# Two transformer blocks on one core: weight splits moved ahead of the fill matmuls in the second block's mixers, two adds given to GpSimd, opening, norms and dense entry reordered

## What is computed

```python
h = h + 0.5 * rmsnorm(swiglu(rmsnorm(h, g1), w_gu, w_down), g2)
u = rmsnorm(h, mix_pre_g)
qa, ka, va, qb, kb, vb, qc, kc, vc, gl = split(u @ w_in)
oa = neighbourhood_attention(qa, ka, va)             # "na", 8 heads, bias table
ob = sliding_window_attention(rope(qb), rope(kb), vb) # "sw", 8 heads, sink
oc = differential_attention(rope(qc), rope(kc), vc)   # "diff", 4 heads, two maps each
merged = sum_n sigmoid(gl_n + b_gate_n) * (o_n @ w_branch_n)
h = h + rmsnorm(merged @ w_out, mix_post_g)
h = h + 0.5 * rmsnorm(swiglu(rmsnorm(h, g3), ...), g4)
```

## Time and profile before

| | us |
|---|---|
| median of 3 runs | 2783.58 (2783.43 to 2784.21) |
| profiled execution | 2782.96 |
| its span, first to last instruction | 2781.2 |
| PE busy in the span | 2564.1 |
| DVE, ACT, POOL busy | 1798.0, 1398.5, 193.8 |

### The profile page before, as it was taken

One profiled execution on the slowest core, in us unless ns is written; L12 is line 12 of the kernel. 1 busy time (PEld: TensorE's weight loads), 2 busy tenths in 40 slices (PEclk: granted clock), 3 DMA queues, 4 the chain that ended last, 5 costly groups with the idle time before them and its releaser, 6 DMA issues. The chain is left out here.

```text
span 2781.2 us, 32412 instructions
## 1 busy us (share of the span) xinstructions
PE 2564.1 (92%) x11950; PEld 2103.3 (76%) x11950; DVE 1798.0 (65%) x1716; ACT 1398.5 (50%) x1485; POOL 193.8 (7%) x270
## 2 busy tenths in 40 slices
PE   7899998699999999999799879889999998888998
PEld 5678776588888888888688767668878876766786
DVE  4564555588888988989654557765555455666553
ACT  3444444376767776777444435444444444443442
POOL 2100020000000000000230000010015000000100
PEclk9899998699999999999899989999999999999999
DMA  6355442289888988999575333345447533333551
GB/s 233 123 189 186 176 149 92 107 344 361 347 351 339 366 349 345 360 355 354 195 236 197 111 133 129 115 167 212 181 166 241 199 129 137 122 122 142 205 188 61
DMA packets 88119, 592.12 MB, mean 213 GB/s; under 512 B 11288, under 2 KB 11472, under 8 KB 20304
## 3 DMA queue, kind: packets, MB, share of 16 engines
q1 hardware_dynamic: 77456, 558.99, 53.0%
q0 software_dynamic: 10560, 31.74, 4.1%
HBM read 585.36 MB, written 5.32 MB: 212 GB/s over the span
## 5 line engine op out<-in xcount | busy, mean ns | idle before, releaser
L566 PE MATMUL pp<-hi_a,uT_hi 128*128 128x512 f32 x2224 | 901.3, 405 | 48.0 <-DVE uT_lo L1733 22.1
L568 PE MATMUL pp<-hi_a,uT_lo 128*128 128x512 f32 x2224 | 877.4, 395 | 0.0
L567 PE MATMUL pp<-lo_a,uT_hi 128*128 128x512 f32 x2224 | 877.3, 394 | 0.0
L1814 DVE TENSOR_TENSOR lo_a<-raw_a,hi_a 128x2048 fp32r<-128x2048 f32 x282 | 652.9, 2316 | 126.5 <-ACT hi_a L1297 126.5
L1297 ACT ACTIVATE hi_a<-raw_a 128x2048 fp32r<-128x2048 f32 x282 | 537.8, 1908 | 6.4 <-DMA raw_a<-in_moe_gu 5.9
L566 PEld LDWEIGHTS pp<-hi_a,uT_hi 128*128 128x128 f32 x2224 | 427.2, 192 | 138.0 <-issue 27.8
L568 PEld LDWEIGHTS pp<-hi_a,uT_lo 128*128 128x128 f32 x2224 | 426.0, 192 | 92.3
L567 PEld LDWEIGHTS pp<-lo_a,uT_hi 128*128 128x128 f32 x2224 | 428.0, 192 | 82.4
L567 PE MATMUL acc<-lo_b,hT_hi 128*128 128x512 f32 x792 | 311.9, 394 | 0.0
L1847 DVE TENSOR_TENSOR lo_b<-raw_b,hi_b 128x2048 fp32r<-128x2048 f32 x116 | 265.9, 2292 | 46.4 <-ACT hi_b L1315 45.3
L566 PE MATMUL acc<-hi_b,hT_hi 128*128 128x512 f32 x576 | 227.8, 395 | 10.8 <-DVE lo_b L1847 10.8
(11 more groups left out here) (251 smaller groups left out, 2806.7 us busy)
## 6 DMA issues: line engine op xcount, KB each, us to landing
raw_a<-in_moe_gu SPq DMA_DIRECT2D x176, 1024.0 KB, 6.3
raw_b<-in_moe_wd SPq DMA_DIRECT2D x88, 1024.0 KB, 8.4
raw_a<-in_ffn_w_gu SPq DMA_DIRECT2D x88, 1024.0 KB, 6.7
raw_a<-in_w_in SPq DMA_DIRECT2D x72, 1024.0 KB, 6.8
raw_b<-in_ffn_w_down SPq DMA_DIRECT2D x44, 1024.0 KB, 4.9
raw_a<-in_ffn_gu SPq DMA_DIRECT2D x22, 1024.0 KB, 5.9
raw_a<-in_w_out SPq DMA_DIRECT2D x16, 1024.0 KB, 5.9
raw_a<-in_w_branch SPq DMA_DIRECT2D x12, 1024.0 KB, 5.9
```

The lines of the kernel that those rows point to most:

```text
L566: nc.tensor.matmul(out_ap, l_hi, r_hi, start=start, stop=False, skip_group_check=True)
L567: nc.tensor.matmul(out_ap, l_hi, r_lo, start=False, stop=False, skip_group_check=True)
L568: return nc.tensor.matmul(out_ap, l_lo, r_hi, start=False, stop=stop, skip_group_check=True)
L1814: ins = nc.vector.tensor_tensor(lo_a[:, slot, cs], raw_a[:, slot, cs], hi_a[:, slot, cs].bitcast(F32), ALU.subtract)
```

## The change

1. **Tables.** `va` comes before `qk1` in `MIX`, `UNITS` is dealt out anew, and the splits move to other items and stand ahead of the item's units (the number in `SPLIT` says how many units stay ahead of them). The rotations of `kb`, `qb`, `qc`, `kc` come one item earlier and stand ahead of the item's units on DVE.

```diff
-MIX = (("in", "qk0", 512, 0), ("in", "qk1", 512, 512), ("in", "va", 512, 1024), ("in", "kb", 256, 1536),
+MIX = (("in", "qk0", 512, 0), ("in", "va", 512, 1024), ("in", "qk1", 512, 512), ("in", "kb", 256, 1536),
-UNITS = {"na": (1, 1, 1, ((3, 2), (2, 0), (2, 0), (2, 0), (2, 0), (2, 0), (2, 0), (2, 0))),
-         "sw": (1, 1, 1, ((1, 1),) * 8), "diff": (1, 1, 2, ((2, 1), (2, 2), (2, 1), (2, 1)))}
-SPLIT = {"na": (0, 1, 2, 4, 6), "sw": (0, 1, 3, 5, 7), "diff": (0, 1, 2, 3)}
-ROTATE = {"na": {5: "kb", 6: "qb"}, "sw": {2: "qc", 4: "kc"}, "diff": {}}
+UNITS = {"na": (1, 1, 1, ((2, 1), (2, 0), (2, 1), (2, 0), (2, 1), (2, 0), (2, 0), (2, 0))),
+         "sw": (1, 1, 2, ((0, 1),) + ((1, 1),) * 7), "diff": (1, 1, 2, ((2, 1), (2, 2), (2, 1), (2, 0)))}
+SPLIT = {"na": {1: 0, 2: 0, 4: 0, 6: 0, 7: 0}, "sw": {0: 0, 2: 0, 4: 0, 6: 0, 7: 1},
+         "diff": {0: 0, 1: 0, 2: 2, 3: 1}}
+ROTATE = {"na": {4: "kb", 5: "qb"}, "sw": {1: "qc", 3: "kc"}, "diff": {}}
```

In ACT's `mix` (DVE's `item` is changed alike):

```diff
-                        units(UNITS[kind][3][it][part])
+                        todo = UNITS[kind][3][it][part]
                         if part == 0 and it in SPLIT[kind]:
+                            units(SPLIT[kind][it])
+                            todo -= SPLIT[kind][it]
                             split()
+                        units(todo)
```

```diff
                     if kind == "diff":
-                        ins = nc.vector.tensor_scalar(s_o_, s_in, SCALE, None, ALU.mult)
+                        nc.vector.tensor_reduce(negmax[:, M % 4, :], s_in, AX_X, ALU.max, negate=True).then_inc(s_nm, 1)
+                        signal(s_sc)
+                        return
...
+                    src = acc[:, M % 2, tt * S:(tt + 1) * S] if kind == "diff" else sc[:, M % 2, tt, :]
```

```diff
                             if which:
                                 dve.wait_ge(s_fev, n["fev"])
-                                link(nc.vector.tensor_tensor(merged[:, tt, cs], merged[:, tt, cs], t[:, tt, cs], ALU.add))
+                                signal(s_part)
...
+                    g.wait_ge(s_part, n["added"])
+                    nc.gpsimd.tensor_tensor(merged[:, tt, cs], merged[:, tt, cs], t[:, tt, cs], ALU.add) \
+                      .then_inc(s_added, 1)
```

```diff
+                dve.wait_ge(s_ss, n["ss"])
+                link(nc.vector.tensor_tensor(merged[:, tt, :].rearrange("p (h c) -> p h c", h=2),
+                                             acc[:, 2 * tt:2 * tt + 2, :],
+                                             vec[:, slot, :].rearrange("p (h c) -> p h c", h=2), ALU.mult))
...
+                link(nc.vector.scalar_tensor_tensor(out=x[:, tt, :], in0=merged[:, tt, :], scalar=rstd[:, tt:tt + 1],
+                                                    in1=x[:, tt, :], op0=ALU.mult, op1=ALU.add))
```

```diff
+                        if opening and tt == 1:
+                            turn(Chunk(c.half, c.rest - 1))
...
-                    turn(Chunk(0, 0))
+                    if experts > 1:
+                        turn(Chunk(0, 0))
```

More of the change, by code:

```diff
@@ L530, in _ @@
             for i in range(N_LAYERS):
-                for j in range(2 if i else 0, D_IN // 512):
+                for j in range(2 if i else 1, D_IN // 512):
                     weight(wide(a["w_in"][i], 512 * j))
@@ L686, in gate_up @@
                     pe.wait_ge(s_alo, c.at(a0 + 1))
+                    opening = experts == 1 and isinstance(j, int) and j == 1
                     if c.rest == 0:
@@ L825, in qk @@
                     M = m0 + m
-                    if M >= 2:
+                    if kind == "diff" and m >= 2:
+                        pe.wait_ge(s_exp, n["exp"] + m - 1)
+                    elif M >= 2:
                         pe.wait_ge(s_sc, M - 1)
@@ L1396, in sb_sigmoids, with attend @@
                 nc.scalar.activation(z, z, ACT.Sigmoid).then_inc(s_keep, 1)
-            def attend(kind, between, behind, item):
+            def attend(kind, between, behind, item, turned=None):
                 maps = MAPS[kind]
@@ L1445, in attend @@
                 n["item"] += items
+                if kind == "diff":
+                    n["comb"] += items
             def mixer(l):
@@ L1978, in across, with attend @@
                 lo_tile(1, True)
-            def attend(kind, dst, ahead, item, done=None):
+            def attend(kind, dst, ahead, item, done=None, opening=None, early=None):
                 maps = MAPS[kind]
@@ L2089, in attend @@
                             scores(per * (it + 1) + m)
+                    if early and it < TT:
+                        early(it)
+                    if it + 1 < items:
                         if kind == "diff":
@@ L2314, in turn, with mix @@
                     rotate(projected(which)[1], 2 if which == "kb" else 8, which == "qb")
-                def mix(kind, dst, first=None, beside=None, done=None):
+                def mix(kind, dst, first=None, turned=None, done=None):
                     def ahead():
@@ L2335, in item @@
                                 signal(s_rope)
+                        units(todo)
                     n["g"] += 4
                     units(UNITS[kind][0])
-                    attend(kind, dst, ahead, item, done)
+                    attend(kind, dst, ahead, item, done, lambda: units(UNITS[kind][1]), turned)
                 def lambdas():
+                    link(nc.vector.tensor_scalar(pre_q, pre_rstd, SCALE, None, ALU.mult))
                     dve.wait_ge(s_lam, 80 * (l + 1))
@@ L2387, in mixer @@
                 link(nc.vector.tensor_scalar(nlam, nlam, -lam_init, None, ALU.add))
-                mix("diff", mixb[:, :, 1280:1792], beside=diff_beside, done=head_squares)
-                units(1)
+                mix("diff", mixb[:, :, 1280:1792], turned=lo_turned, done=head_squares)
+                wait_rstd()
+                gains["heads"] = gain()
+                for tt in range(TT):
+                    for h in range(3):
+                        head_norm(tt, h)
                 wait_rstd()
@@ L2393, in mixer @@
                     signal(s_rows)
-                for tt in range(TT):
-                    lo_turned(tt)
+                lo_half(1)
+                units(2)
+                lo_turned(0)
                 units(1)
                 signal(s_vecused)
+                lo_turned(1)
                 units(1)
```

198 lines of the change are left out of this document (113 added, 85 removed).

## The result

| | before | after |
|---|---|---|
| median us | 2783.51 (4 runs, 2781.55 to 2784.21) | 2697.42 (4 runs, see below) |
| profiled execution us, span | 2782.96, 2781.2 | 2695.91, 2693.9 |
| ratio after to before | | 0.969, interval 0.9671 to 0.9709 |

One of the four executions after was disturbed and took 14324.09 us: it counts in the median alone, while the ratio is that of the other three (2695.74 to 2698.93, the middle one 2695.91).

A forecast was written before the change was run, and what follows sets the result against it. PE was taken to bound the kernel, leaving its idle 217 us and low clock to win. Mixers 38, opening 5.1, norms 5.2 and dense entry 4.4 sum to 52.7, giving 2730.9 us, range 2712 to 2758.

The forecast's parts named there:

- The mixers: Second block's two mixers: of 54 us to win in each, 35.2 stay, so two give 38 us.
- the opening: Program start: PE starts its first weights 8.9 us earlier, of which 5.1 us are kept.
- norms: Between stages: less work behind the root, 0.9 us five times and some 0.85 at the end, 5.2 us.
- dense entry: Dense networks: PE's 1.1 us waits for tile 1's hidden rows go, in two networks by half, 4.4 us.
- The waits left: In each mixer after the change: 23.6 us of listed waits plus 4.6 of waits below 1 us.
- replay: Mixers' new order gone through item by item with durations of before; found 23.6 us of waits for each mixer.
- The clock: In each mixer: low clock behind waits of about 3 us and more costs 12 us before, 7 after.
- The adds: Mixer's end: tile 0's last add on POOL waits for a `lo` half; rows are out 3.0 us late.
- the bias's time: Opening: POOL's masked bias, at 40.6 us before, becomes the next wait and should be there at about 37.5.
- POOL and DVE do shut each other out: Rival, mixers: each of eight adds holds a `lo` half 1.3 us and waits 2.3; 2753 us, chance 0.12.
- Evictions behind splits: Rival, mixers: DVE evicts behind the split, so PE's next unit may wait; 12 for each mixer, 2755 us, chance 0.14.
- The pair's copy behind the split: Rival, mixers: ACT's split ahead of the copy makes DVE's scores late; 17 more for each mixer, 2803 us, chance 0.08.

The follow-up runs named there:

- The early mask: The changed kernel, but POOL starts loading the first layer's mask ahead of its copies of the bias rows; 0.9658, 2688.1 us.
- the undone norm: The changed kernel, but the RMS norm behind a mixer and a network takes its two DVE instructions behind the root again; 0.9717, 2704.5 us.

## Why the prediction was right or wrong

**The mixers, forecast 38, measured 75.** The mechanism and the place were right, the size of what is left was not: I had 35.2 us of waits and clock left in each mixer, and 18.0 and 23.5 were left. This is more than the whole miss, as the opening gave 3.3 us less than forecast, and norms and dense entry 0.8 more. Two terms failed.
- *The waits left.* I had 23.6 us by replay and 4.6 for small waits, 28.2 for each mixer. From the stretches, length less busy time between head 0's product and `merged`, it is 16.3 and 14.2. Nearly every wait of the list is there, at its item and with its releaser, and nearly all are shorter: na's item 3 1.7 (forecast 2.3), its seventh weight 3.05 (4.9), sw's first turn 1.6 (2.0), item 1 0.35 (1.1), item 3 2.1 (3.6), item 7 0.9 (1.4), diff's 0.6 (2.9), the adds' 1.0 (3.0). Longer were the second turn of the tail, 1.1 (0.4), and in one mixer sw's item 5 (2.8 and 0.7, forecast 2.0). The list's 23.6 us are 15.2 and 13.2. A part of the error shows in the item that the forecast reckons in full, na's item 4: from its first transposes at 1597.81 ACT is through with the exponentials after 3.3 us, the split after 7.0, the pair's copy after 8.0 (forecast 3.4, 7.1, 8.4), and PE has 10.1 us of work (9.8). So the replay gave PE 0.3 too little to do and ACT 0.4 too much, 0.7 together, about the error of na's item 3, sw's turn and its items 1 and 7 (0.4 to 0.8); for the larger errors, of 1.5 to 2.3 us, the cause stays open. Then 4.6 us for small waits were added, where only some 1 was found (the tail's first turn 0.7, a second wait of 0.4 in diff).
- *The clock.* I took 12 us as its cost before and 7 after, so 5 back for each mixer. PE's busy time for the same matmuls fell by 13.1 and 6.6. Before, the granted clock was at its low level for 41.0 us of each mixer, and PE busy for 28.4 of them, of which about half, 14.2, is the cost (matmuls start every 0.42 us there, every 0.23 at the full clock); after, it was low for 3.4 and 20.5 us, with PE busy for 3.4 and 18.6: 1.7 and 9.3. So the 12 was 2 short, and the 7 lies between two mixers of nearly the same waits, one of which paid almost nothing. The forecast priced the clock by counting waits of about 3 us and more. That fits the seven of the mixer before (2.8 us and more), but not the kernel after: the same wait of 1.74 us in na's item 3 left the clock high in the first mixer and had the low level behind it in the second. PE alone, with clock, DMA share and GB/s:

```profile
1591.15:1595.15 4.00, 4.00 (x28) 1.00 0.32 84
2262.10:2265.50 3.40, 3.40 (x17) 0.50 0.56 169
```

The seventh weight's wait shows how far the replay could be used all the same. ACT, DVE and PE at na's last item:

```profile
1619.71 3.70 ACT L1285 ACTIVATE hi_a<-raw_a 128x2048 fp32r<-128x2048 f32 x2
...
1621.64 4.49 DVE L2289 TENSOR_TENSOR lo_a<-raw_a,hi_a 128x2048 fp32r<-128x2048 f32 x2 [2.97 <-ACT hi_a L1285]
...
1626.19 0.50 PE L581 MATMUL pp<-hi_a,uT_hi 128*128 128x512 f32 x1 [3.05 <-DVE lo_a L2289]
```

The cause was the forecast's: the split stands behind item 6's exponentials. Moved one item ahead, it took this wait away.

**The adds, forecast 3.0 us of wait in each tail.** A wait of 1.0 was there, and the tail is 1.5 us shorter without the adds on POOL. The direction of the block was wrong: POOL, DVE and PE at the write of tile 0's last piece:

```profile
1790.55 1.27 POOL L2638 TENSOR_TENSOR merged<-merged,t 128x512 f32<-128x512 f32 x1 [2.88 <-DVEq L1733]
...
1790.56 3.40 DVE L2289 TENSOR_TENSOR lo_a<-raw_a,hi_a 128x2048 fp32r<-128x2048 f32 x1
...
1791.92 1.09 PE L593 MATMUL tp<-ident,merged 128*128 128x128 f32 x8 [1.04 <-POOLq L2642]
```

The add starts 10 ns ahead of the `lo` half and takes its 1.27 us undisturbed; the half takes 3.40 instead of 2.29, so it waited for the add. I had let the add wait for the half; nor was the add before still under way. The rule of the Trainium skill (SBUF — State Buffer, Who interferes with whom), that the two exclude each other for the whole instruction, agrees with the trace: 3.40 - 2.29 = 1.1 us, nearly the add's length.

**The opening, forecast 5.1, measured 1.8** (and nothing in the second trace of the same kernel, where the transposes came at 155.4 as before). PE started at 12.63 (forecast 12.3), 8.5 us earlier. The step that failed is the bias's time: I took 37.5, and POOL's add ended at 39.6, behind three loads that wait for each other (POOL waited 6.80 us for the rows' way through DRAM, 6.92 for the mask, 6.49 for the bias). The mask's wait did get shorter (9.47 before), but the bias's own load took 2.0 us longer than before's 4.49, so the add began at 38.36 against 38.52:

```profile
38.36 1.25 POOL L2608 TENSOR_TENSOR bias<-bias,mask 128x512 f32<-128x512 f32 x1 [6.49 <-DMA bias<-chunk_bias_rows]
...
42.52 0.66 PE L874 MATMUL acc<-ident,sc 128*128 128x128 f32 x4 [4.44 <-ACT sc L1412]
```

2.9 us of the lead were left at 42.52 (before, this instruction came at 45.43). The second thing I left out: behind the wait of 4.44 us PE does its next two units at a mean clock of 0.76. 27 matmuls there and 27 of a later pair of units:

```profile
42.93:50.10 7.17, 7.17 (x27) 0.76 0.59 121
55.74:61.30 5.56, 5.56 (x27) 1.00 0.43 50
```

That is 1.6 us more, and 1.3 are left. The early mask, with which nearly the whole lead is kept, shows that this chain was what held the opening back.

**Norms, forecast 5.2**: the trace of the undone norm holds 5.5 us of waits and 7.8 of length. The waits were forecast right; that the rest is clock was not shown. **Dense entry, forecast 4.4**: 4.2 in the networks, of which 3.2 is idle time. Right in the main. Four of the five networks are shorter than before, the first block's is not (198.5 before, 199.0 after, with 0.4 us less idle time at a clock of 0.97 against 0.98).

**The rivals.** POOL and DVE do shut each other out, at 1.9 us for each mixer, not 11. Evictions behind splits cost 0.4 to 0.9 us each, nowhere more. The pair's copy behind the split is the largest wait left in sw (2.1 and 2.8), far from the 5.0 in all eight places that would have turned the sign.

## What to carry to other kernels

Cut a stage at the work that paces it, and read idle time and clock for each stretch: a mean clock of 0.94 hid 0.80 beside 1.00, and over both mixers 55.3 us of waits took 19.7 us of busy time with them. In an order written by hand, how the units of filler and the slow side jobs are dealt out over the items counted most here (26 us), and where a side job stands within its item about a third of that. Undoing one table at a time showed where most of the waits had gone (48 of 56 us). A small serial chain of loads on a quiet queue can eat the lead that a faster start gives: look for what was hidden just behind the wait that is being removed.

## What the runs showed of the hardware

- Equal waits do not give an equal clock. With the same program and 4.8 us idle in na each time, na took 58.99 us (0.97) in one mixer and 61.50 (0.92) in the next; with the adds on DVE 58.98 and 57.38 (1.00). The row of that last one:

```profile
2242.47:2299.85 57.38, 52.58 (x309) 1.00 0.43 159
```

  The two mixers of that execution differ by 4.9 us, the one with less idle time being the longer; before, they differed by 0.1. That is about the spread of the changed kernel's runs (2689.7 to 2698.9), which is wider than that of before (2780.3 to 2784.5), and it sets what one profile can tell here. Why the clock answers so differently stays open.
- An add of POOL that begins first is not slowed by DVE's two-input subtraction, and delays it by nearly its own length (1.27 against 1.1 us). At 1760.12 two adds took 4.57 us together and the two subtractions beside them 5.87 (4.49 alone): the first add took 1.28, the second, which began at 1761.37 beside a subtraction under way since 1760.96, 3.31. So whichever began first had its way, in both directions.
